# The second mixer's windowed attention: two heads at a time in the row and column halves of TensorE

## The chip, the cores and the metric

The kernel runs on one core of one Trainium2 chip. The metric is the time of one execution on the device, in microseconds (us). A core has TensorE (matrix products, PE in the profile), VectorE (DVE), ScalarE (ACT), GpSimd (POOL) and SyncE (SP, which here only issues the loads of weights). Each engine runs its instructions in its own order and waits on semaphores for the others. Operands lie in SBUF, matrix products are written to PSUM, which has 8 banks of 512 float32 columns on 128 partitions.

## What is computed

A two-layer hybrid backbone over 512 latent tokens and 256 context tokens, width 1024, in float32. Each layer is a gated feed-forward block, a mixer and a second feed-forward block, each modulated and residual. Layer 0's mixer is a Mamba-2 scan beside a dense multi-head attention. Layer 1's mixer, the one this case is about, is a windowed attention: 16 query heads and 4 key/value heads of width 64, a window of 128 tokens to either side, all 256 context keys, and one learned logit ("sink") per head in the softmax.

```python
def window_attend(q, k, v, kc, vc, sink, scale):
    # q (b,n,hk,r,d), k/v (b,n,hk,d), kc/vc (b,lc,hk,d), sink (hk,r); blocks of QBLK = 128 queries
    band = jnp.abs(qi[:, None] + WINDOW - kj[None, :]) <= WINDOW
    def block(i):
        ...
        s_loc = jnp.einsum("bqhrd,bkhd->bhrqk", qb, kb).astype(F32) * scale
        s_loc = jnp.where(valid, s_loc, -jnp.inf)
        s_ctx = jnp.einsum("bqhrd,bkhd->bhrqk", qb, kc).astype(F32) * scale
        prob = jax.nn.softmax(jnp.concatenate([s_loc, s_ctx, sink_l], axis=-1), axis=-1)
        return (jnp.einsum("bhrqk,bkhd->bqhrd", prob[..., :span], vb)
                + jnp.einsum("bhrqk,bkhd->bqhrd", prob[..., span:span + lc], vc))
```

## The kernel before

The program is written out engine by engine, in one fixed order of stages: feed-forward, first mixer (projection items, dense attention, scan), feed-forward twice, second mixer, feed-forward, output. The order in each engine's queue is the order in which the functions are called for that engine, and every dependence is a semaphore written by hand. Activations lie with their features on the partitions: a tile of 128 features x 768 tokens (512 latent, then 256 context).

The second mixer has four steps. `pe_items`, `act_items` and `dve_items` make keys (`gk`, 2 blocks of 128 features, so two heads to a block) and queries (`gq`, 8 blocks) with their norms and the rotary embedding; `pe_v_o` makes the values `gv` with tokens on the partitions; `pe_attend`, `act_attend` and `dve_attend` do the attention; `pe_out` is the output projection, which waits until all of the attention's outputs are written. GpSimd and SyncE have nothing to do in the attention.

The attention runs over 64 units: 16 heads x 4 blocks of 128 queries, `qt` = 0 to 3. A unit of `qt` 1 or 2 reads 640 keys (256 of the context and three blocks of 128), here called a middle unit; one of `qt` 0 or 3 reads 512, an edge unit. A query block of `gq` holds head i in partitions 0 to 63 and head i + 4 in 64 to 127, as their key heads lie in `gk`. The two halves are not used together: each unit takes one head.

For unit q the work goes round all three engines:

- TensorE, L1213: scores, 64 partitions contracted, into one of two pairs of PSUM banks. A float32 product stands in the profile as two records.
- VectorE, L1268: adds one or two masks of 128 columns to the scores; L1272: the row maximum; L1276 and L1278: scale, compare with the sink, negate.
- ScalarE, L1242: the exponential with its row sum, into `prob`; L1246: the exponential of the sink.
- VectorE, L1288, L1291, L1293: sum, reciprocal, scaling of `prob`.
- TensorE, L1222: four or five transposes of 128 x 128 into a pair of banks; ScalarE, L1259: one copy of them to `probT`.
- TensorE, L1231: the values, 64 columns out, into one half of the partitions of bank 6 or 7; ScalarE, L1252: rounded copy `go_hi`; VectorE, L1299: remainder `go_lo`.

The three engines hold four units at a time. In its turn q, TensorE issues the scores of q, the transposes of q-2 and the values of q-3. ScalarE issues the exponential of q, the sink of q, `go_hi` of q-3 and the copy of q-2. VectorE issues masks, maximum and the two small operations of q, then the sum, reciprocal and scaling of q-1, then `go_lo` of q-3.

## Time and profile before

| | |
|---|---|
| median of 3 runs | 3572.6 us (3569.13 to 3574.8) |
| the profiled execution's own time | 3573.73 us |
| its span, first to last instruction | 3571.9 us |
| mean granted TensorE clock | 0.971 |
| TensorE, VectorE, ScalarE, GpSimd busy | 94%, 47%, 28%, 8% of the span |

The span is the profiled execution; 1.8 us of its time lie around it. The page lists busy time by engine, the span in 40 slices, the DMA queues, the chain of work that ended last, and the costliest groups of instructions. "L1213" is line 1213 of the kernel before. In a timeline a row is one instruction, or several alike in a row (x5), with its start and its duration from first start to last end.

### The profile page before, as it was taken

What the parts mean: (1) busy time and instruction counts of PE and PEld (TensorE: products, weight loads), DVE (VectorE), ACT (ScalarE), POOL (GpSimd) and SP (SyncE); (2) the same over time, 40 slices, a digit from 0 to 9 for tenths busy, and PEclk for the clock granted to TensorE, in tenths of its full rate; (3) what the DMA queues carried; (4) which work ended last, traced back from release to release, by engine and by line L of the source; (5) the groups of instructions that cost most, each with busy time, mean ns of one, the idle gap of its engine ahead of it and who ended that gap; (6) DMA issues with size and microseconds to landing.
All of it is one profiled execution on the core that took longest, in us unless ns stands there. A gap on an engine that the chain in (4) does not pass through costs nothing.

```text
span 3571.9 us, 44734 instructions
## 1 busy us (share of the span) xinstructions
PE 3366.4 (94%) x18291; PEld 3039.5 (85%) x18291; DVE 1663.5 (47%) x2539; ACT 988.7 (28%) x1477; POOL 272.9 (8%) x310
## 2 busy tenths in 40 slices
PE   4999999989999989989999999999999988889999
PEld 3999999976779875578999999999999866668887
DVE  5643526435443626646623255432235457743333
ACT  2211212355431311133112113211212435532222
POOL 0100000200000015621000001000000000000000
PEclk9999999999999999999999999999999989999999
DMA  4533424401013210013523242322233210023332
GB/s 168 153 112 95 124 65 130 124 26 49 1 49 88 61 46 1 1 30 115 156 59 99 67 134 61 100 80 62 61 93 108 62 37 1 1 60 100 89 94 94
DMA packets 390047, 272.92 MB, mean 76 GB/s; under 512 B 33922, under 2 KB 365945, under 8 KB 389753
## 3 DMA queue, kind: packets, MB, share of 16 engines
q1 hardware_dynamic: 364537, 182.50, 17.7%
q0 software_dynamic: 25344, 88.09, 8.0%
q8 instruction: 119, 1.95, 0.2%
q14 instruction: 47, 0.39, 0.0%
HBM read 262.16 MB, written 8.39 MB: 76 GB/s over the span
## 4 chain that ended last, share of the span: by engine, by line
PE 52%; DVE 3%; ACT 2%; issue 1%; POOL 0%; ACTq 0%; DVEq 0%
PE ps L448 46%; PE ps L656 1%; PE ps L1213 1%; DVE stat L1272 1%; PE ps L1231 1%; PE ps L1585 1%; PE ps L1222 1%; PE ps L1100 1%; ACT prob L1242 0%; DVE ps L1268 0%; POOL xs L1628 0%; DVE w_lo L438 0%; ACT probT L1259 0%; PE ps L1559 0%; DVE h_sb L896 0%
## 5 line engine op out<-in xcount | busy, mean ns | idle before, releaser
L448 PE MATMUL ps<-u_hi,w_hi 128*128 128x384 f32 (+2 forms) x2992 | 833.0, 348 | 43.9 <-DVE w_lo L438 24.6
L438 DVE TENSOR_TENSOR w_lo<-ring,w_hi 128x1024 fp32r<-128x1024 f32 (+3 forms) x357 | 414.9, 1165 | 900.4 <-ACT w_hi L423 707.6
L448 PE MATMUL ps<-u_lo,w_hi 128*128 128x384 f32 (+2 forms) x2992 | 824.8, 345 | 0.0
L448 PE MATMUL ps<-u_hi,w_lo 128*128 128x384 f32 (+2 forms) x2992 | 824.0, 345 | 0.0
L448 PEld LDWEIGHTS ps<-u_hi,w_hi 128*128 128x128 f32 x2992 | 544.3, 191 | 74.7 <-issue 47.0
L448 PEld LDWEIGHTS ps<-u_lo,w_hi 128*128 128x128 f32 x2992 | 544.9, 190 | 22.6 <-issue 1.7
L448 PEld LDWEIGHTS ps<-u_hi,w_lo 128*128 128x128 f32 x2992 | 544.2, 190 | 21.5
L423 ACT CAST w_hi<-ring 128x1024 fp32r<-128x1024 f32 (+3 forms) x229 | 221.5, 968 | 1052.5 <-PE ps L448 1004.1
L448 PE MATMUL ps<-hid_hi,w_hi 128*128 128x384 f32 (+1 forms) x1232 | 343.6, 349 | 0.0
L448 PE MATMUL ps<-hid_lo,w_hi 128*128 128x384 f32 (+1 forms) x1232 | 342.9, 348 | 0.0
L448 PE MATMUL ps<-hid_hi,w_lo 128*128 128x384 f32 (+1 forms) x1232 | 342.0, 347 | 0.0
L626 DVE SCALAR_TENSOR_TENSOR m_sum<-m_in,sc,m_sum 128x1024 f32<-128x1024 f32 x224 | 277.1, 1279 | 6.0 <-DMA m_in<-in_w_mod 5.9
L430 ACT CAST w_hi<-ring 128x1024 fp32r<-128x1024 f32 x128 | 134.2, 1049 | 375.8 <-PE ps L448 375.8
L448 PEld LDWEIGHTS ps<-hid_lo,w_hi 128*128 128x128 f32 x1232 | 229.4, 192 | 6.8
L448 PEld LDWEIGHTS ps<-hid_hi,w_lo 128*128 128x128 f32 x1232 | 229.1, 192 | 6.8
L448 PEld LDWEIGHTS ps<-hid_hi,w_hi 128*128 128x128 f32 x1232 | 228.3, 192 | 6.9
L777 DVE TENSOR_TENSOR hid_f<-hid_f,ps 128x768 f32<-128x768 f32 x66 | 63.0, 955 | 313.0 <-PE ps L448 310.1
L896 DVE SCALAR_TENSOR_TENSOR h_sb<-ps,mod,h_sb 128x384 f32<-128x384 f32 (+3 forms) x296 | 135.1, 506 | 130.3 <-PE ps L448 130.1
L620 POOL DMA_DIRECT2D m_in<-in_w_mod x128 | 67.9, 530 | 1563.3 <-DVE m_sum L626 749.8
L758 ACT ACTIVATE hid_f<-ps 128x768 f32<-128x768 f32 x66 | 53.8, 815 | 431.9 <-PE ps L448 431.9
L1242 ACT ACTIVATE prob<-ps,stat 128x768 f32<-128x768 f32 (+3 forms) x112 | 83.9, 749 | 186.4 <-DVE stat L1278 105.5
L1222 PE MATMUL ps<-cst,prob 128*128 128x128 f32 x512 | 78.1, 281 | 34.4 <-ACT probT L1259 33.5
(250 smaller groups left out, 3678.0 us busy)
## 6 DMA issues: line engine op xcount, KB each, us to landing
ring<-in_w_ff_in SPq DMA_DIRECT2D x176, 512.0 KB, 3.8
m_in<-in_w_mod POOLq DMA_DIRECT2D x128, 512.0 KB, 4.0
ring<-in_w_ff_out SPq DMA_DIRECT2D x64, 512.0 KB, 3.6
ring<-in_w_in_e SPq DMA_DIRECT2D x26, 512.0 KB, 3.8
ring<-in_w_ff_out SPq DMA_DIRECT2D x32, 384.0 KB, 3.1
m_first<-in_w_mod POOLq DMA_DIRECT2D x16, 512.0 KB, 12.0
ring<-in_w_out_e SPq DMA_DIRECT2D x16, 512.0 KB, 3.7
...
```

The costliest lines, as they stand in the source:

```text
L423: act.copy(w_hi[:, (n % 2) * SLOT:(n % 2) * SLOT + WIDE[n]], ring[:, (n % RING) * SLOT:(n % RING) * SLOT + WIDE[n]]).then_inc(w_split_hi, 1)
L430: act.copy(w_hi[:, (n % 2) * SLOT:(n % 2) * SLOT + SLOT], ring[:, (n % RING) * SLOT:(n % RING) * SLOT + SLOT]).then_inc(w_split_hi, 1)
L438: dve.tensor_tensor(w_lo[:, b:b + WIDE[n]], ring[:, s:s + WIDE[n]], w_hi[:, b:b + WIDE[n]], ALU.subtract).then_inc(w_split_lo, 1)
L448: mm = pe.matmul(ps_at(p, c0, c1) if halved else pair(p)[:, c0:c1], w, x[:, c0:c1], start=start and i == 0, stop=stop and i == 2)
L620: pool.dma_start(m_in[:, D * (n % 2):D * (n % 2) + D], mod_src(x, k)).then_inc(m_full[n % 2], 16)
L626: x = dve.scalar_tensor_tensor(out=at_, in0=w, scalar=by, in1=at_, op0=ALU.mult, op1=ALU.add)
L656: mm = pe.matmul(bank(first + slot_, c0, c0 + 1), m_sum[:, D * (2 * slot_ + s) + P * d:D * (2 * slot_ + s) + P * d + P], ones[:, 0:1], sta ...
L758: act.activation(two(hid_f[:, jj, :]), halves(jj), ACT.Silu).then_inc(f_silu, 1)
L777: return dve.tensor_tensor(two(hid_f[:, q, :]), two(hid_f[:, q, :]), halves(2 + q), ALU.mult)
L896: x = dve.scalar_tensor_tensor(out=h[:, d, t0:t1], in0=pair(d % 2)[:, t0:t1] if whole else ps_at(d % 2, t0, t1), scalar=mod_group(g)[:, 2, ...
L1222: mm = pe.transpose(pair(2)[:, P * k:P * k + P], prob[:, i % 3, P * k:P * k + P], ident)
L1242: act.activation(prob[:, q % 3, :x["n"]], pair(q % 2, 1024)[:, :x["n"]], ACT.Exp, bias=stat[:, 4 + q % 4:5 + q % 4], scale=x["scale"], acc ...
```

## The change

The attention of the second mixer gets functions of its own. It takes two heads at a time, x = 0 to 7 being heads 2x and 2x + 1, which share a key head (x // 2), so there are 32 units `WU` instead of 64, each with 640 or 512 keys for each of its two heads:

- `gq` is loaded with its blocks in plain order, so one transfer for a block instead of two; head 2x lies in partitions 0 to 63, head 2x + 1 in 64 to 127.
- `gk` has four blocks: each holds one key head twice, in both halves of the partitions. GpSimd makes the copies (`pool_keys`), six of 64 x 768.
- `pe_window`: score products alternate between the halves, head 0 from rows 0 to 63, head 1 from rows 64 to 127. A unit's scores take three banks (two sets of three for two units). The tables `tiles`, `order` and `first` lay the columns so that products of both halves that follow each other write different banks; where both write the middle bank, one waits for the other (`wn_tail`).
- The transposes of both heads (8 or 10) go in rounds of four through one bank, bank 6, which ScalarE empties after each round. Between the rounds TensorE issues products with the values, alternating between the column halves 0 to 63 and 64 to 127, into one bank, bank 7.
- `act_window`: a unit's copies to `gpt` (2 or 3), then an exponential for each head, one for both sinks, then one `go_hi` of 128 x 128.
- `dve_window`: one addition of the masks for both heads (2 x 128 or 2 x 256 columns), one maximum over both heads' scores, the small operations on two columns, the scaling of the first head's probabilities alone, and one `go_lo` of 128 x 128.
- `pool_window`: GpSimd scales the second head's probabilities.

TensorE in the steady state, two turns before (`at_ex` is signalled by the exponential, `at_pn` by the scaling, `at_pt` by the copy `probT`, `at_o` by `go_lo`):

```order
L1213 MATMUL ps<-gk,gq 128x256 [waits at_ex]
L1213 MATMUL ps<-gk,gq 128x256
L1213 MATMUL ps<-gk,gq 128x128
L1222 MATMUL ps<-cst,prob 128x128 [waits at_pt,at_pn]
L1222 MATMUL ps<-cst,prob 128x128 x3
L1231 MATMUL ps<-probT,gv 64x128 [waits at_o,at_pt]
L1231 MATMUL ps<-probT,gv 64x128 x4
L1213 MATMUL ps<-gk,gq 128x256 [waits at_ex]
```

The transposes of a unit stand in one block, with one wait for a copy. One turn of the change (`wn_pt` by a copy to `gpt`, `wn_lo` by `go_lo`, `wn_n0` and `wn_n1` by the scalings of VectorE and GpSimd):

```order
L1321 MATMUL ps<-gk,gq 128x256 [waits wn_ex]
L1321 MATMUL ps<-gk,gq 128x256 x3
L1344 MATMUL ps<-cst,gp 128x128 [waits wn_n0,wn_pt,wn_lo]
L1344 MATMUL ps<-cst,gp 128x128 x3
L1357 MATMUL ps<-gpt,gv 64x128 x4
L1344 MATMUL ps<-cst,gp 128x128 [waits wn_pt,wn_n1]
L1344 MATMUL ps<-cst,gp 128x128 x3
L1357 MATMUL ps<-gpt,gv 64x128 x4
L1344 MATMUL ps<-cst,gp 128x128 [waits wn_pt]
L1344 MATMUL ps<-cst,gp 128x128
L1321 MATMUL ps<-gk,gq 128x256 [waits wn_ex]
```

The transposes of a unit, one block before, now stand in two or three blocks with values between them, and each block waits for a copy of ScalarE. The first of them also waits for the `go_lo` of the turn before.

ScalarE in the steady state, one turn before (middle unit; the first row is the exponential):

```order
L1242 ACTIVATE prob,stat<-ps,stat 128x640 [waits at_tr,at_nm]
L1246 ACTIVATE stat<-sink,stat 128x1
L1252 CAST go_hi<-ps 64x128 [waits at_pv]
L1259 COPY probT<-ps 128x512 [waits at_pv,at_tr]
L1242 ACTIVATE prob,stat<-ps,stat 128x640 [waits at_tr,at_nm]
```

One copy stands behind `go_hi`. The same in the change (the copies come before the exponentials of the turn):

```order
L1372 COPY gpt<-ps 128x512 [waits wn_pv,wn_tr]
L1372 COPY gpt<-ps 128x512 [waits wn_tr]
L1372 COPY gpt<-ps 128x256 [waits wn_tr]
L1381 ACTIVATE gp,gst<-ps,gst 128x512 [waits wn_tr,wn_nm]
L1381 ACTIVATE gp,gst<-ps,gst 128x512
L1385 ACTIVATE gst<-gst 128x2 [waits wn_sk]
L1389 CAST go_hi<-ps 128x128 [waits wn_pv]
```

The single copy behind `go_hi` has become two or three copies ahead of two exponentials, each of which waits for a round of transposes.

The diff's core. In the tables of loads and keys:

```diff
-        gq, gk, gv = at("gq", 16 * T, 8 * T), at("gk", 24 * T, 2 * T), at("gv", 26 * T, NT * 256)
+        gq, gk, gv = at("gq", 16 * T, 8 * T), at("gk", 24 * T, 4 * T), at("gv", 28 * T, NT * 256)
...
-            c0 = HD * (8 * (i // 4) + i % 4)
-            return lambda s: [(slot(s, 8)[:, :, 64 * e:64 * e + 64],
-                               w_ino[:, :, c0 + 4 * HD * e:c0 + 4 * HD * e + 64]) for e in range(2)]
+            return block(w_ino, 0, 8, P * i)
...
-            pe_attend(pe, n_mla, len(units))
-            pe.wait_ge(at_o, len(units))
+            pe.wait_ge(kk_two, 6)
+            pe_window(pe)
+            pe.wait_ge(wn_lo, NWU)
...
             pool_squares(pool, 4)
+            pool_keys(pool)
+            pool_window(pool)
             pool_squares(pool, 5)
```

The new functions:

```diff
+        for x in range(8):
+            for qt in range(SEQ // P):
+                lo, hi = max(0, qt - 1), min(3, qt + 1)
+                if hi - lo == 2:
+                    tiles = ([4, 5, qt - 1, qt + 1, qt], [qt, 4, 5, qt - 1, qt + 1])
+                    order = [(0, 4, 1), (1, 1, 2), (0, 0, 2), (1, 3, 1), (0, 2, 1), (1, 4, 1), (0, 3, 1), (1, 0, 1)]
+                    first, mask = (0, 896), (256, C_MP, 256)
+                else:
+                    tiles = ([4, 5, lo, hi], [4, 5, lo, hi])
+                    order = [(0, 0, 2), (1, 0, 2), (0, 2, 2), (1, 2, 2)]
...
+        def pool_keys(pool):
+
+            for b in range(2):
+                pool.wait_ge(hn_fin, items[n_even + b]["nrope"] + 1)
+                pool.wait_ge(hn_n, items[n_even + b]["norm"] + 1)
+                for e in range(2):
+                    pool.tensor_copy(gk[64 * e:64 * e + 64, 2 * b + 1, :], gk[64:128, 2 * b, :]).then_inc(kk_two, 1)
+                pool.wait_ge(kk_two, 3 * b + 2)
+                pool.tensor_copy(gk[64:128, 2 * b, :], gk[0:64, 2 * b, :]).then_inc(kk_two, 1)
+
+        def pool_window(pool):
+            for u in range(NWU):
+                n = WU[u]["n"]
+                pool.wait_ge(wn_ri, u + 1)
+                pool.tensor_scalar(gp[:, u % 3, n:2 * n], gp[:, u % 3, n:2 * n], gst[:, u % 4, 6, 1:2], None,
+                                   ALU.mult).then_inc(wn_n1, 1)
...
+        def pe_window(pe):
+            for u in range(NWU + 3):
+                if u < NWU:
+                    x = WU[u]
+                    g, q0 = x["g"], x["q0"]
+                    if u >= 2:
+                        pe.wait_ge(wn_ex, 2 * u - 2)
+                    for e, j, m in x["order"]:
+                        c = x["first"][e] + P * j
+                        k0 = P * x["tiles"][e][j]
+                        r = slice(64 * e, 64 * e + 64)
+                        if x["tail"] and (e, j) == (1, 0):
+                            pe.wait_ge(wn_tail, x["tail"])
+                        mm = pe.matmul(win(u, c, c + P * m), gq[r, x["x"], q0:q0 + P], gk[r, g, k0:k0 + P * m],
+                                       start=True, stop=True)
+                        if x["tail"] and (e, j) == (0, 4):
+                            mm.then_inc(wn_tail, 1)
+                    mm.then_inc(wn_sc, 1)
+                todo = list(range(WU[u - 3]["n"] // P)) if u >= 3 else []
+                if todo:
+                    y = WU[u - 3]
+                    pe.wait_ge(wn_pt, y["r0"] + y["nr"])
+                    if u >= 4:
+                        pe.wait_ge(wn_lo, u - 3)
+                i = u - 2
+                if 0 <= i < NWU:
+                    x = WU[i]
+                    nt = 2 * x["n"] // P
+                    for r in range(x["nr"]):
+                        if r == 0:
+                            pe.wait_ge(wn_n0, i + 1)
+                        if 4 * r + 4 > nt // 2 and (r == 0 or 4 * r <= nt // 2):
+                            pe.wait_ge(wn_n1, i + 1)
+                        if x["r0"] + r:
+                            pe.wait_ge(wn_pt, x["r0"] + r)
+                        for k in range(4 * r, min(nt, 4 * r + 4)):
+                            mm = pe.transpose(bank(6)[:, P * (k % 4):P * (k % 4) + P], gp[:, i % 3, P * k:P * k + P], ident)
+                        mm.then_inc(wn_tr, 1)
+                        if r < x["nr"] - 1:
+                            pe_window_values(pe, u - 3, todo[:2])
+                            todo = todo[2:]
...
+        def pe_window_values(pe, u, js):
+            for j in js:
+                y = WU[u]
+                nk = y["n"] // P
+                for e in range(2):
+                    k, c = y["tiles"][e][j], y["n"] * e + P * j
+                    mm = pe.matmul(bank(7)[64 * e:64 * e + 64, 0:P], gv[:, k, HD * y["g"]:HD * y["g"] + HD],
+                                   gpt[:, u % 2, c:c + P], start=j == 0, stop=j == nk - 1)
+                if j == nk - 1:
+                    mm.then_inc(wn_pv, 1)
+
+        def act_window(act):
+            for u in range(NWU + 3):
+                i = u - 2
+                if 0 <= i < NWU:
+                    x = WU[i]
+                    for r in range(x["nr"]):
+                        act.wait_ge(wn_tr, x["r0"] + r + 1)
+                        if r == 0 and i >= 2:
+                            act.wait_ge(wn_pv, i - 1)
+                        c0, c1 = 512 * r, min(2 * x["n"], 512 * r + 512)
+                        act.copy(gpt[:, i % 2, c0:c1], bank(6)[:, 0:c1 - c0]).then_inc(wn_pt, 1)
+                if u < NWU:
+                    x = WU[u]
+                    n = x["n"]
+                    act.wait_ge(wn_nm, u + 1)
+                    if u >= 3:
+                        act.wait_ge(wn_tr, WU[u - 3]["r0"] + WU[u - 3]["nr"])
+                    for e in range(2):
+                        c = x["first"][e]
+                        act.activation(gp[:, u % 3, n * e:n * e + n], win(u, c, c + n), ACT.Exp,
+                                       bias=gst[:, u % 4, 2, e:e + 1], scale=HD ** -0.5,
+                                       accum_out=gst[:, u % 4, 4, e:e + 1]).then_inc(wn_ex, 1)
+                    act.wait_ge(wn_sk, u + 1)
+                    act.activation(gst[:, u % 4, 5, :], gst[:, u % 4, 3, :], ACT.Exp).then_inc(wn_es, 1)
+                if u >= 3:
+                    y = WU[u - 3]
...
+        def dve_window(dve):
+            for u in range(NWU + 3):
+                if u < NWU:
+                    x = WU[u]
+                    f = gst[:, u % 4]
+                    dve.wait_ge(wn_sc, u + 1)
+                    c0, mk, w = x["mask"]
+                    s = win(u, 0, 1536).rearrange("p (b n) -> p b n", n=512)[:, 0:3:2, c0:c0 + w]
+                    dve.tensor_tensor(s, c_(mk, w).rearrange("p (o n) -> p o n", o=1).broadcast_to([P, 2, w]), s,
+                                      ALU.add).then_inc(wn_mk, 1)
+                    dve.wait_ge(wn_mk, u + 1)
+                    c = x["first"][1]
+                    s = win(u, 0, 2 * c).rearrange("p (b n) -> p b n", n=c)[:, :, 0:x["n"]]
+                    dve.tensor_reduce(f[:, 0, :], s, AX, ALU.max).then_inc(wn_mx, 1)
+                    sk = sink[:, 2 * x["x"]:2 * x["x"] + 2]
+                    dve.wait_ge(wn_mx, u + 1)
+                    dve.scalar_tensor_tensor(out=f[:, 1, :], in0=f[:, 0, :], scalar=HD ** -0.5, in1=sk,
+                                             op0=ALU.mult, op1=ALU.max).then_inc(wn_m, 1)
+                    dve.wait_ge(wn_m, u + 1)
+                    dve.tensor_scalar(f[:, 2, :], f[:, 1, :], -1.0, None, ALU.mult).then_inc(wn_nm, 1)
+                    dve.tensor_tensor(f[:, 3, :], sk, f[:, 1, :], ALU.subtract).then_inc(wn_sk, 1)
+                i = u - 1
+                if 0 <= i < NWU:
+                    f, n = gst[:, i % 4], WU[i]["n"]
+                    dve.wait_ge(wn_ex, 2 * i + 2)
+                    dve.wait_ge(wn_es, i + 1)
+                    dve.tensor_tensor(f[:, 4, :], f[:, 4, :], f[:, 5, :], ALU.add).then_inc(wn_l, 1)
+                    dve.wait_ge(wn_l, i + 1)
+                    dve.reciprocal(f[:, 6, :], f[:, 4, :]).then_inc(wn_ri, 1)
+                    dve.wait_ge(wn_ri, i + 1)
+                    dve.tensor_scalar(gp[:, i % 3, 0:n], gp[:, i % 3, 0:n], f[:, 6, 0:1], None, ALU.mult).then_inc(wn_n0, 1)
+                if u >= 3:
+                    y = WU[u - 3]
+                    o = slice(y["q0"], y["q0"] + P)
+                    dve.wait_ge(wn_hi, u - 2)
+                    dve.tensor_tensor(go_lo[:, y["x"], o], bank(7, 0, P), go_hi[:, y["x"], o], ALU.subtract).then_inc(wn_lo, 1)
```

## Rows read from the trace of the kernel before

**Rows 1.** The page: busy time and share of the span, chain by line

```profile
PE 3366.4 (94%) x18291; PEld 3039.5 (85%) x18291; DVE 1663.5 (47%) x2539; ACT 988.7 (28%) x1477; POOL 272.9 (8%) x310
...
PE ps L448 46%; PE ps L656 1%; PE ps L1213 1%; DVE stat L1272 1%; PE ps L1231 1%; PE ps L1585 1%; PE ps L1222 1%; PE ps L1100 1%; ACT prob L1242 0%; DVE ps L1268 0%; POOL xs L1628 0%; DVE w_lo L438 0%; ACT probT L1259 0%; PE ps L1559 0%; DVE h_sb L896 0%
```

**Rows 2.** The tiles gq and go_lo: first and last score product, first and last output

```profile
L1213 PE MATMUL ps<-gk,gq x320: 269/376/793, 2916.4 to 3131.7; 64*128 64x256 f32 x128, 64*128 64x128 f32 x32
...
L1299 DVE TENSOR_TENSOR go_lo<-ps,go_hi x64: 282/288/295, 2929.7 to 3143.2; 64x128 fp32r<-64x128 f32 x64
```

**Rows 3.** Chain of waits, 2890 to 3160 us: start us, us, what

```profile
by line: PE ps L1213 12.1%; DVE stat L1272 11.9%; PE ps L1231 11.8%; issue 10.8%; PE ps L1222 7.2%; PE ps L1100 7.0%; ACT prob L1242 6.4%; DVE ps L1268 6.3%; PE ps L448 6.2%; ACT probT L1259 4.3%; DVE stat L1276 3.3%; ACT go_hi L1252 3.2%; 
...
3001.05 1.24 PE ps L1231 x10
...
3055.26 1.24 PE ps L1231 x10
```

**Rows 4.** Timeline, one middle unit: start us, us, engine, line, op, operands

```profile
3005.43 0.80 ACT L1242 ACTIVATE prob<-ps,stat 128x640 f32<-128x640 f32 x1 [2.00 <-DVE stat L1278]
...
3006.22 0.28 ACT L1246 ACTIVATE stat<-sink,stat 128x1 f32<-128x1 f32 x1
3006.52 0.26 ACT L1252 CAST go_hi<-ps 64x128 fp32r<-64x128 f32 x1
3006.81 0.59 ACT L1259 COPY probT<-ps 128x512 f32<-128x512 f32 x1
3006.82 0.29 DVE L1299 TENSOR_TENSOR go_lo<-ps,go_hi 64x128 fp32r<-64x128 f32 x1 [0.62 <-ACT go_hi L1252]
3007.14 0.49 DVE L1268 TENSOR_TENSOR ps<-cst,ps 128x128 f32<-128x128 f32 x2
...
3007.54 0.63 PE L1222 MATMUL ps<-cst,prob 128*128 128x128 f32 x4 [0.82 <-ACT probT L1259]
3007.67 0.82 DVE L1272 TENSOR_REDUCE stat<-ps 128x1 f32<-128x640 f32 x1
...
3008.10 1.09 PE L1231 MATMUL ps<-probT,gv 128*64 128x128 f32 x8
3008.53 0.21 DVE L1276 TENSOR_SCALAR stat<-stat,sink 128x1 f32<-128x1 f32 x1
...
3008.96 0.80 ACT L1242 ACTIVATE prob<-ps,stat 128x640 f32<-128x640 f32 x1 [1.57 <-DVE stat L1278]
```

**Rows 5.** Groups by line and form, 2950 to 3100 us: busy us, mean ns

```profile
L1272 DVE TENSOR_REDUCE stat<-ps 128x1 f32<-128x640 f32 x23 | 19.0, 824 | 0.8
...
L1272 DVE TENSOR_REDUCE stat<-ps 128x1 f32<-128x512 f32 x22 | 15.2, 691 | 0.8
...
L1242 ACT ACTIVATE prob<-ps,stat 128x512 f32<-128x512 f32 x22 | 15.1, 688 | 29.4 <-DVE stat L1278 29.4
```

**Rows 6.** Timeline of TensorE in the SSD stage, heads in both column halves

```profile
1361.88 0.42 PE L1585 MATMUL ps<-ee,st 128*64 128x128 f32 x1
1361.94 0.42 PE L1585 MATMUL ps<-mf,xdt 128*64 128x128 f32 x1
1362.10 0.42 PE L1585 MATMUL ps<-ee,st 128*64 128x128 f32 x1
1362.16 0.42 PE L1585 MATMUL ps<-ee,xdt 128*64 128x128 f32 x1
```

**Rows 7.** Stretches: from:to, us, busy us (count) of each engine, PEclk, DMA

```profile
1360.70:1364.10 3.40, 3.40 (x29) 3.40 (x28) 2.73 (x4) 0.00 (x0) 0.37 (x1) 0.50 0.00 0
...
1537.00:1558.00 21.00, 12.74 (x43) 7.01 (x42) 9.80 (x11) 12.36 (x15) 6.92 (x4) 1.00 0.00 0
2915.00:2934.00 19.00, 16.89 (x53) 12.37 (x54) 12.16 (x40) 6.34 (x18) 0.00 (x0) 0.56 0.01 3
2934.00:3140.00 206.00, 179.21 (x1120) 137.72 (x1119) 152.17 (x507) 108.23 (x299) 0.00 (x0) 1.00 0.00 1
```

**Rows 8.** Groups by line and form, GpSimd, whole span

```profile
L499 POOL TENSOR_TENSOR acc<-acc,sqn 128x512 f32<-128x512 f32 x5 | 6.4, 1288 | 18.7 <-ACT sqn L490 18.7
```

84 lines of the change are left out of this document (33 added, 51 removed).

## The prediction

> **What bounds the kernel now.** The page comes first [rows 1]. TensorE is busy for 94% of the span, and the chain that ended last is made of its dense products (L448, 46%); VectorE is at 47%. That is an average over stages, and says nothing of the stage that changes. Its ends are in [rows 2]: the first score product starts at 2916.4 us, the last `go_lo` at 3143.2, and 0.3 later it ends, so the attention takes 227.1 us, 6% of the span. The output projection waits for it, so each microsecond gained there is one of the end.
>
> In that stage the chain goes from engine to engine [rows 3]: scores 12.1%, maximum 11.9%, values 11.8%, transposes 7.2%, exponential 6.4%, with the masks, copies and small operations between them. From 3001.05 to 3055.26 the pattern repeats after 16 units: 54.21 us, 3.39 us a unit. 64 units make 216.8 us, and filling, emptying and the first products at a low clock make the other 10.3.
>
> One middle unit shows what the 3.39 consist of [rows 4]. From exponential to exponential: the exponential starts at 3005.43, the sink 0.79 later, `go_hi` 0.30 later, `go_lo` 0.30, the masks 0.32, the maximum 0.53, L1276 0.86, and the next exponential 0.43 later, at 3008.96. That is 3.53 us without a gap: ScalarE waits for VectorE's maximum, VectorE for ScalarE's `go_hi`. The same sum for an edge unit is 3.09, and the mean of both 3.31 against 3.39 measured, so this way of adding is some 2% short. TensorE is close behind the loop: busy for 179.21 of 206 us [rows 7].
>
> **What the change removes and adds, per pair of heads.** Two old units cost 6.78 us. The work that is now done once for two heads, from the nearest rows:
>
> - Masks, one operation of 512 columns (middle) or 256 (edge). A subtraction from PSUM takes 0.29 us for 128 columns (`go_lo` [rows 4]), and the maximum 0.133 more for each further 128 [rows 5]: 0.69 for 512 and 0.42 for 256. Before, two pairs of 0.49 (middle).
> - Maximum over 1280 or 1024 columns. 0.691 for 512 and 0.824 for 640 [rows 5] give 1.04 ns a column: 1.49 and 1.22 us. Only the fixed part of one is saved.
> - Two small operations, the sink's exponential, `go_hi` and `go_lo`, each once instead of twice, at 0.15 to 0.30 each [rows 4]. I take the same price for the wider forms: two masks on 128 partitions take 0.49 together, no more than two `go_lo` on 64 would [rows 4]. The other bound is twice these, some +1 us a pair; no row speaks for it.
> - The exponentials stay two: 2 x 0.79 (middle) or 2 x 0.68 (edge, from 0.688 [rows 5]).
>
> This gives a first leg, from the start of `go_hi` to the next exponential over VectorE: middle 0.30 + 0.32 + 0.73 + 1.53 + 0.43 = 3.31 us, edge 0.30 + 0.32 + 0.46 + 1.26 + 0.43 = 2.77 (0.04 is the gap behind each of masks and maximum).
>
> **The wait that takes its place.** Before, one copy of 0.59 us (edge) emptied the transposes, and it stood off the loop. Now all pass one bank in rounds of four, and ScalarE must do the two or three copies before it may do the turn's exponentials. The first round waits on TensorE for `go_lo` of the turn before. So there is a second leg from the same `go_hi`: `go_lo` starts 0.30 later and takes 0.29; a product of TensorE starts 0.14 behind the copy that it waits for (3006.81 + 0.59 to 3007.54 [rows 4]); four transposes take 0.63; 0.04 to the copy; the copy of 512 columns takes 0.59 [rows 4]. To here 1.99 us. A second round is 0.14 + 0.67 + 0.59 = 1.40, and a third of two transposes and 256 columns 0.14 + 0.45 + 0.37 = 0.96, where 0.37 is 0.59 less twice the 0.11 by which exponentials of 640 and 512 columns differ [rows 4, 5]. The leg takes 3.39 us where the copies are those of an edge pair and 4.35 for a middle pair. It is longer than the first leg each time, so ScalarE now waits for transposes and not for the maximum.
>
> A turn is this leg, two exponentials and 0.30 for the sink. The copies belong to the pair two before the one whose exponentials come next, so the four kinds of turn are: edge exponentials, edge copies 1.66 + 3.39 = 5.05; middle, edge 1.88 + 3.39 = 5.27; middle, middle 1.88 + 4.35 = 6.23; edge, middle 1.66 + 4.35 = 6.01. Together 22.56 us for four pairs, 5.64 a pair, and 180.5 for 32.
>
> Both ends: the pipeline is three turns deep as before, and 10.3 us stood there. The turns are longer and fewer, the low clock at the start stays; I take 7, between 4 (no low clock) and 10.3. **The stage takes 187 us instead of 227, 40 less.**
>
> **TensorE in a turn.** Column halves overlap in the scan's stage [rows 6]: L1585 makes heads in both halves, and products of two chains alternate there while each chain advances by 0.22 us, at the low clock (1360.70 to 1364.10, PEclk 0.50 [rows 7]). One chain alone, the values L1231, takes 1.09 us for eight records at the full clock [rows 4], 0.11 to 0.12 each once the last has started, and twice that at the low one. So the second chain is free. I take the same for the row halves, which no row shows: scores 1.1 us, values 10 records of two at 0.11, transposes 1.1, and six changes of shape of about 0.1: 3.9 us in a middle turn of 5.3 to 6.2. That is off the bound.
>
> The Trainium skill, "TensorE: Matmul & The Clock Gate", part 3, says that small products in different row groups start within 4 ns of each other and run together, as those in different column groups do; no row here has it for rows. By that rule the sum is the same.
>
> **GpSimd.** Its scaling of 640 columns has one input where GpSimd's addition has two, which takes 1.29 us for 512 columns [rows 8]: between half of that and 1.29 x 640 / 512 = 1.61 us. It is needed only by the second round of transposes a turn later, so it costs nothing. The six copies of keys, 768 columns, take at most 1.5 x 1.29 = 1.9 each and run under the projection of the queries, where GpSimd is idle; cost 0, at most some 2 us if VectorE is held up. The loads of `gq` become one transfer for two; SyncE's queue there waits for slots, not for data: 0. Outside the attention nothing else moves.
>
> **The sum.** 3573.7 - 40 = 3533.7 for the profiled execution. The median shown is 1.1 lower, which gives **3533 us**.
>
> **Rivals.**
>
> 1. *The row halves, or both kinds, run one after another.* TensorE then needs 2.2 for scores, 1.1 for transposes, 2.2 for values and 0.6 for changes of shape, 6.1 us in a middle pair and 5.0 in an edge pair, about what the turns have. Each block of values between rounds takes 0.87 + 0.2 instead of 0.43 + 0.2, 0.1 us beyond the copy it lies under, and the scores come later for the masks. Some 9 us: 3542. Against it stand [rows 6], for columns only.
> 2. *VectorE and GpSimd hold each other up.* Both scalings start at the same reciprocal. No row shows VectorE slowed by GpSimd. If it waits out a whole scaling of up to 1.61 us, the slack between the small operations and `go_lo` (1.88 + 0.30 + 0.18, less 1.1 of its own work, so 1.2) leaves up to 0.4 us a turn, 12 us: 3545. The Trainium skill, "SBUF — State Buffer", section "Summary: rules for kernel authors", speaks for this: of a VectorE instruction in a two-port mode and GpSimd, the second to issue is blocked until the first ends. By it VectorE, which waits for its own signal, would mostly go first.
> 3. *The clock stays low through the stage.* The row of 2915 to 2934 has PEclk 0.56, one of 1.2 GHz for most of it, at the same thin start of the pipeline. TensorE would need 2.1 for scores, 2.1 for transposes, 2.1 for values and 0.6 for changes of shape, 6.9 us in a middle pair and 5.7 in an edge pair, and part of each wait for a round's copy comes on top: about 6.8 a pair, 218 and the ends 7, 225 us: 3571, no difference. Against it: from 1537 to 1558 TensorE is busy for 12.74 of 21 us and keeps the full clock [rows 7]; the turns above give 3.9 of 5.6, more than that.
> 4. *The other side: each change of half costs what a change of shape costs.* The values start 0.56 after four transposes of 0.11 [rows 4], so a change of shape costs 0.12. A middle pair has 7 changes of half in its scores and 9 in its values, an edge pair 3 and 7. With nothing overlapped TensorE needs 6.1 + 1.9 = 8.0 and 5.0 + 1.2 = 6.2 us, 7.1 a pair, 227 us, and with ends 234: 3580, slower. It decides from 0.10 us a change on, where TensorE's 5.55 + 13 x 0.10 passes the old time of a pair. Against it: in [rows 6] an alternation costs nothing.
>
> **How the numbers follow.** Forecast 0.73; rival 1 0.09; rival 2 0.07; rival 3 0.05; rival 4 0.03; 0.03 for a stage shorter than 178 us, if rounds hand over faster than 0.14 + 0.04. 0.2% of this kernel, 7 us, is about what a measurement can tell from no change. Faster takes all but rivals 3 and 4 and a bit more: 0.91; within 0.2% 0.06; slower 0.03. The forecast's own range is the 2% of the sum in either direction, 3 to 6 us at the ends and 2 for the keys: 3526 to 3541. Reaching to rivals 1 and 2: 3524 to 3547.
>
> **What the profile afterwards would show.** The attention from its first score to its last `go_lo` takes 183 to 191 us. Four pairs (two heads, all queries) repeat every 22.6 us. ScalarE's copies to `gpt` wait for TensorE's transposes, about 0.8 us before each second copy, and the exponentials wait little for `gst`. Maximum 1.22 and 1.49 us, masks 0.42 and 0.69. Score products of one half start while the other's run. GpSimd's scaling is under 1.6 us. Wrong would be: exponentials that wait for the maximum (then the first leg binds, and the price of the rounds is smaller than I say), scores of a middle pair taking 2.2 us (rival 1), VectorE's scaling much over half a microsecond (rival 2), PEclk at 0.5 past the first 20 us (rival 3).

## The result, and the profile after

The changed kernel takes **3520.24 us** (median of 4 runs, 3519.51 to 3522.98) beside 3570.86 (4 runs, 3567.36 to 3574.8) for the kernel before. The ratio is 0.9859, with a 95% interval of 0.9842 to 0.9876. That is 51 us less where 40 were forecast, and below the low end of the range, 3524. The profiled execution took 3522.98, its span 3520.8.

The page of the kernel after, the rows that answer to [rows 1]: busy time by engine, and the chain that ended last, by line.

```profile
PE 3303.5 (94%) x18355; PEld 2983.3 (85%) x18355; DVE 1604.3 (46%) x2283; ACT 971.2 (28%) x1429; POOL 344.9 (10%) x348
...
PE ps L457 72%; PE ps L1193 2%; PE ps L665 2%; PE ps L1711 1%; PE ps L1344 1%; PE ps L1211 1%; PE ps L1109 1%; PE ps L1321 1%; ACT gpt L1372 1%; DVE w_lo L447 1%; PE ps L1685 1%; PE ps L1202 1%; DMA u_sb<-in_ctx 1%; PE ps L1004 1%; PE ps L1686 1%
```

In the chain the new stage's transposes L1344, scores L1321 and copies L1372 have 1% each; the page says no more of one stage. The tiles `gq` and `go_lo` give its ends, as in [rows 2] (engine, operation, count: shortest, median and longest ns, first and last start).

```profile
L1321 PE MATMUL ps<-gk,gq x384: 269/376/792, 2916.6 to 3074.4; 64*128 64x128 f32 x98, 64*128 64x256 f32 x94
```

```profile
L1426 DVE TENSOR_TENSOR go_lo<-ps,go_hi x32: 290/292/293, 2934.9 to 3092.0; 128x128 fp32r<-128x128 f32 x32
```

From 2916.6 to 3092.3 the attention takes **175.7 us**, where it took 227.1 and I had forecast 187. The spans differ by 51.1 and the stage by 51.4: everything happened inside the stage, and it also began at the same time (2916.4 and 2916.6), so the keys' copies and the new loads cost nothing that shows.

The chain of waits, 2890 to 3110 us, by line, answers to [rows 3]:

```profile
by line: PE ps L1344 22.8%; issue 16.4%; PE ps L1321 14.3%; ACT gpt L1372 12.7%; PE ps L1109 8.5%; PE ps L457 8.1%; PE ps L1357 5.6%; ACT gp L1381 4.9%; DVE go_lo L1426 1.5%; ACT go_hi L1389 1.0%; DVE gv L1161 0.9%; DVE gst L1404 0.6%; DVE 
```

Before, the maximum stood at the head with the scores and values (11.9%). Now it has 0.6%, and the transposes with their copies have 35.5%. The list of waits for 2940 to 3080 us (engine, line and what it waited for: us in total, times, longest) says the same from the other side:

```profile
ACT gpt L1372 <- PE ps L1344: 58.2, 67, 1.1
```

ScalarE stands 58.2 of 140 us before its copies. No wait of the exponential L1381 for the maximum is in the list. One turn, from exponential to exponential, answers to [rows 4]; both its exponentials and its copies are those of edge pairs:

```profile
3001.38 0.69 ACT L1381 ACTIVATE gp<-ps,gst 128x512 f32<-128x512 f32 x1
...
3002.05 0.69 ACT L1381 ACTIVATE gp<-ps,gst 128x512 f32<-128x512 f32 x1
...
3002.72 0.21 ACT L1385 ACTIVATE gst<-gst 128x2 f32<-128x2 f32 x1
3002.81 0.27 ACT L1389 CAST go_hi<-ps 128x128 fp32r<-128x128 f32 x1
3003.11 0.29 DVE L1426 TENSOR_TENSOR go_lo<-ps,go_hi 128x128 fp32r<-128x128 f32 x1 [2.43 <-ACT go_hi L1389]
...
3003.50 0.63 PE L1344 MATMUL ps<-cst,gp 128*128 128x128 f32 x4 [0.76 <-issue]
3004.04 1.49 DVE L1404 TENSOR_REDUCE gst<-ps 128x2 f32<-128x1280 f32 x1
...
3004.17 0.58 ACT L1372 COPY gpt<-ps 128x512 f32<-128x512 f32 x1 [1.09 <-PE ps L1344]
...
3004.90 0.63 PE L1344 MATMUL ps<-cst,gp 128*128 128x128 f32 x4 [0.18 <-ACT gpt L1372]
...
3005.56 0.59 ACT L1372 COPY gpt<-ps 128x512 f32<-128x512 f32 x1 [0.81 <-PE ps L1344]
3005.76 0.17 DVE L1410 TENSOR_SCALAR gst<-gst 128x2 f32<-128x2 f32 x1
...
3006.05 0.80 ACT L1381 ACTIVATE gp<-ps,gst 128x640 f32<-128x640 f32 x1
```

Against the forecast's turn of 5.05 us:

| step, from start to start | forecast | measured |
|---|---|---|
| two exponentials, to the sink | 1.36 | 1.34 |
| sink to `go_hi` | 0.30 | 0.09 |
| `go_hi` to the first transposes | 0.73 | 0.69 |
| transposes to copy | 0.67 | 0.67 |
| copy to the second round's transposes | 0.73 | 0.73 |
| transposes to copy | 0.67 | 0.66 |
| last copy to the next exponential | 0.59 | 0.49 |
| sum | 5.05 | 4.67 |

The other three kinds of turn, read in the same way, take 4.88 (forecast 5.27), 5.78 (6.23) and 5.57 (6.01). Four pairs take 20.89 us instead of 22.56; over 32 pairs that is 13.4 us. The ends took 8.6 us instead of 7. The difference, 11.8, is what the stage was shorter than the forecast's 187.5.

The wide operations, by line and form from 2950 to 3080 us (busy us, mean ns | idle before), answer to [rows 5] and [rows 8]; the last fence is GpSimd:

```profile
L1404 DVE TENSOR_REDUCE gst<-ps 128x2 f32<-128x1280 f32 x12 | 17.9, 1490 | 0.4
L1404 DVE TENSOR_REDUCE gst<-ps 128x2 f32<-128x1024 f32 x13 | 15.9, 1224 | 0.4
L1399 DVE TENSOR_TENSOR ps<-cst,ps 128x512 f32<-128x512 f32 x12 | 8.2, 685 | 0.0
...
L1399 DVE TENSOR_TENSOR ps<-cst,ps 128x256 f32<-128x256 f32 x13 | 5.5, 419 | 0.0
```

```profile
L1305 POOL TENSOR_SCALAR gp<-gp,gst 128x640 f32<-128x640 f32 x14 | 31.4, 2242 | 35.9 <-DVE gst L1419 35.9
L1305 POOL TENSOR_SCALAR gp<-gp,gst 128x512 f32<-128x512 f32 x12 | 22.3, 1856 | 45.4 <-DVE gst L1419 45.4
```

Maximum 1490 and 1224 ns, masks 685 and 419: the forecast had 1.49, 1.22, 0.69 and 0.42. GpSimd needs 2.24 us for 640 columns, outside the bound of 1.61. The stretches (from:to, us, busy us of PE, PEld, DVE, ACT, POOL, then PEclk) answer to [rows 7]:

```profile
2930.00:2940.00 10.00, 8.28 (x77) 5.67 (x76) 4.90 (x16) 5.88 (x16) 4.10 (x2) 0.94 0.01 2
2940.00:3080.00 140.00, 105.91 (x1040) 74.36 (x1038) 88.53 (x243) 81.81 (x229) 55.00 (x27) 1.00 0.00 1
```

The granted clock stays at 2.4 GHz from 2940 on. TensorE is busy for 105.91 of 140 us, so it has room; that the stage is a chain of handovers is what e3 and b1 put to the test.

### The profile page after: what moved, and what is told of

The parts are those of the page before. It is cut to its first block, busy times and chain, and to the rows that moved or that the text cites. A ratio compares the mean times of both kernels' runs of the same rounds, so it can differ in the third digit from the quotient of the medians.

```text
span 3520.8 us, 44458 instructions
## 1 busy us (share of the span) xinstructions
PE 3303.5 (94%) x18355; PEld 2983.3 (85%) x18355; DVE 1604.3 (46%) x2283; ACT 971.2 (28%) x1429; POOL 344.9 (10%) x348
## 4 chain that ended last, share of the span: by engine, by line
PE 88%; ACT 4%; DVE 4%; issue 2%; POOL 1%; DMA 1%; SPq 1%; ACTq 0%; DVEq 0%
PE ps L457 72%; PE ps L1193 2%; PE ps L665 2%; PE ps L1711 1%; PE ps L1344 1%; PE ps L1211 1%; PE ps L1109 1%; PE ps L1321 1%; ACT gpt L1372 1%; DVE w_lo L447 1%; PE ps L1685 1%; PE ps L1202 1%; DMA u_sb<-in_ctx 1%; PE ps L1004 1%; PE ps L1686 1%
## 5 line engine op out<-in xcount | busy, mean ns | idle before, releaser
L1344 PE MATMUL ps<-cst,gp 128*128 128x128 f32 x288 | 49.7, 293 | 39.1 <-issue 20.1
L1305 POOL TENSOR_SCALAR gp<-gp,gst 128x512 f32<-128x512 f32 (+1 forms) x32 | 65.5, 2048 | 167.8 <-DVE gst L1419 167.8
```

Source lines behind the costliest of these rows:

```text
L1305: pool.tensor_scalar(gp[:, u % 3, n:2 * n], gp[:, u % 3, n:2 * n], gst[:, u % 4, 6, 1:2], None, ALU.mult).then_inc(wn_n1, 1)
L1344: mm = pe.transpose(bank(6)[:, P * (k % 4):P * (k % 4) + P], gp[:, i % 3, P * k:P * k + P], ident)
```

## The experiments

Two questions were open. Is the gain what I said it is, the round of waits ScalarE, TensorE, ScalarE in place of two units' loops, with TensorE's halves overlapping? And why was each turn 0.4 us shorter than its sum? Turn lengths below are for the four kinds in the order edge exponentials with edge copies, middle with edge, middle with middle, edge with middle: after has 4.67, 4.88, 5.78, 5.57 = 20.89. e1 to e4 ran beside one set of runs of the kernel before (median 3572.03), e5 to e7 and b1 beside another (3573.06).

### e1: the scores of both heads in one row half

```diff
-                        r = slice(64 * e, 64 * e + 64)
+                        r = slice(0, 64)
```

The second head's scores are made from the first head's queries; the amount of work is the same.

> Of the kernel after, both heads' score products contract partitions 0 to 63 (the second head's scores are then those of the first; the same instructions, shapes and waits). Theory (the two row halves run together, and TensorE is off the bound): the 16 score records of a middle pair grow from 1.37 us to about 2.2, the stage of 175.5 us grows by 0 to 10 us, since TensorE has slack in a turn. Rival (row halves never overlapped, the shorter stage has another cause): scores stay at 1.37 us and the time stays within 2 us of 3520.

Measured: 3534.81 us, ratio 0.9897 (0.9881 to 0.9914), 14.6 more than the change. Turns 5.15, 5.18, 5.77, 5.57 = 21.67. TensorE's timeline of e1 and, under it, the same row of the kernel after:

```profile
3008.71 2.47 PE L1321 MATMUL ps<-gk,gq 64*128 64x128 f32 x16
```

```profile
3006.26 1.37 PE L1321 MATMUL ps<-gk,gq 64*128 64x128 f32 x16
```

A middle pair's 16 records take 2.47 us in one row half and 1.37 in two. So the row halves do overlap, which no row of before could show. In one half the next record starts 0.11 us after one of 128 columns and 0.22 after one of 256, so the time goes with the columns and not with the number of weight loads; it is the products that overlap. The Trainium skill ("TensorE: Matmul & The Clock Gate", part 3) says so, with about 4 ns between starts, and the single records of the change agree with it: from 3007.02 us on those of the two halves start in pairs, 4 to 7 ns apart, and the pairs 0.11 us apart. From the first start to the last it is 1.10 us in the change and 2.19 in e1, which are the 1.1 and 2.2 that I had; the rows add the last record's own 0.27. The stage grew by more than the 10 us that were expected at most.

Of the stage's 12.7 us (188.4 instead of 175.7), 6.2 are the turns' 0.78 x 8 and 6.2 the filling: the first `go_lo` starts 24.5 us after the first score in e1, and 18.3 in the change. At the start TensorE is at 1.2 GHz for a while. The stretches of e1, and under them those of the change and of e5 (further down), where TensorE does the same as in the change:

```profile
2917.00:2930.00 13.00, 12.23 (x45) 10.23 (x44) 8.18 (x21) 3.98 (x12) 1.85 (x1) 0.50 0.00 0
2930.00:2940.00 10.00, 9.66 (x42) 6.48 (x42) 3.51 (x10) 5.27 (x15) 4.49 (x2) 0.67 0.00 0
```

```profile
2917.00:2930.00 13.00, 10.71 (x61) 8.04 (x58) 9.60 (x23) 6.11 (x17) 4.09 (x2) 0.52 0.00 0
```

```profile
2917.00:2930.00 13.00, 8.30 (x68) 6.49 (x68) 11.05 (x27) 6.27 (x18) 3.52 (x2) 0.87 0.01 3
```

In e1 TensorE is busy there almost without a gap (12.23 of 13 us), so the longer scores lengthen the filling. But the clock has a part in it too: it is back at 2.4 GHz later in e1 than in the change (0.67 against 0.94 for 2930 to 2940), and in e5 it was back early, with 16.2 us of filling. So some 2 us of a filling can differ without any change in TensorE's work, and how the 6.2 divide between scores and clock is not shown.

### e2: the values in one column half as well

```diff
-                    mm = pe.matmul(bank(7)[64 * e:64 * e + 64, 0:P], gv[:, k, HD * y["g"]:HD * y["g"] + HD],
-                                   gpt[:, u % 2, c:c + P], start=j == 0, stop=j == nk - 1)
+                    mm = pe.matmul(bank(7)[0:64, 0:P], gv[:, k, HD * y["g"]:HD * y["g"] + HD],
+                                   gpt[:, u % 2, c:c + P], start=True, stop=True)
```

On top of e1. The values of both heads are written over each other and not summed.

> As e1_rows, and both heads' products with the values go to the column half 0 as well, each product for itself (the sum over the key blocks is left out, and half of the outputs are stale). Theory: values between two rounds of transposes (8 records) grow from 0.66 to about 1.1 us, longer than the copy of 0.59 that they lie under, so each second round comes up to 0.3 us later: with the scores some 5 to 20 us over the kernel after, 3525 to 3540. If the whole gain of the change came from the overlap in the halves (rival), this kernel is back at 3560 to 3571.

Measured: 3552.28 us, ratio 0.9947 (0.993 to 0.9964), 32.0 more than the change. Turns 5.38, 6.04, 6.30, 6.05 = 23.77.

```profile
3002.71 1.99 PE L1321 MATMUL ps<-gk,gq 64*128 64x256 f32 x8
3004.63 0.65 PE L1344 MATMUL ps<-cst,gp 128*128 128x128 f32 x4
3005.21 1.09 PE L1357 MATMUL ps<-gpt,gv 128*64 128x128 f32 x8
3006.23 0.66 PE L1344 MATMUL ps<-cst,gp 128*128 128x128 f32 x4
```

```profile
ACT gpt L1372 <- PE ps L1344: 69.2, 60, 2.0
...
DVE ps L1399 <- PE ps L1321: 12.2, 18, 1.1
```

Eight records of values take 1.09 us instead of 0.66, and each stands between two rounds of transposes: the round's period goes from 1.40 (3003.50 to 3004.90 in the change) to 1.60 (3004.63 to 3006.23). The masks now wait for scores, 12.2 us in all. TensorE, busy for 105.91 us between 2940 and 3080 in the change, is now busy for 137.46 of these 140: it has become the bound of the stage, which the expected 3525 to 3540 did not foresee. In this order of the work the overlap in both halves is worth 32 of the 51 us; without it the change would have gained about 20.

### e3: the wait for `go_lo` behind the first round of transposes

The values of a unit must wait until `go_lo` of the one before has read bank 7. The change has that wait ahead of the transposes, which don't use that bank.

```diff
-                    if u >= 4:
-                        pe.wait_ge(wn_lo, u - 3)
...
+                if j == 0 and u >= 1:
+                    pe.wait_ge(wn_lo, u)
```

> Of the kernel after, TensorE waits for the last go_lo in front of the first product with the values instead of in front of the first round of transposes. Theory (the leg through the rounds sets the turn): the first round runs while go_hi and go_lo are made; the legs go_hi to exponential of now 3.24 us (edge copies) and 4.15 (middle copies) fall to about 3.1 (VectorE's leg) and 3.5, some 1.5 us in four pairs, 12 us in all, up to 16: 3505 to 3509. Rival (VectorE's leg sets the turn, as before the change): no difference, 3520.

Measured: 3506.08 us, ratio 0.9818 (0.9802 to 0.9835), 14.2 less than the change. Turns 4.59, 4.79, 4.95, 4.75 = 19.08; 8 x 1.81 = 14.5. The timeline of e3, one turn:

```profile
3000.36 0.78 ACT L1381 ACTIVATE gp<-ps,gst 128x640 f32<-128x640 f32 x1
...
3000.56 0.63 PE L1342 MATMUL ps<-cst,gp 128*128 128x128 f32 x4 [0.60 <-issue]
...
3001.23 0.26 ACT L1389 CAST go_hi<-ps 128x128 fp32r<-128x128 f32 x1
3001.37 0.60 ACT L1372 COPY gpt<-ps 128x512 f32<-128x512 f32 x1
...
3001.86 0.66 PE L1357 MATMUL ps<-gpt,gv 128*64 128x128 f32 x8 [0.67 <-DVE go_lo L1426]
...
3003.15 0.59 ACT L1372 COPY gpt<-ps 128x512 f32<-128x512 f32 x1 [1.18 <-PE ps L1342]
```

```profile
ACT gpt L1372 <- PE ps L1342: 35.2, 43, 1.2
...
PE ps L1357 <- DVE go_lo L1426: 14.0, 20, 0.7
...
ACT gp L1381 <- DVE gst L1410: 8.2, 13, 0.6
```

The first round's transposes now run during the exponentials, and the copy follows `go_hi` at once. So the leg by `go_lo` and the transposes was indeed what set the turn. Nearly all of the gain lies in the two turns with middle copies (0.83 and 0.82 us); those with edge copies lose only 0.08 and 0.09, because the leg over VectorE's maximum lies right below and takes over. The other leg doesn't vanish either: the second round now stands behind values that wait for `go_lo` (14.0 us), and exponentials that did not wait for the maximum in the change now do (8.2).

### e4: the kernel before, with `go_hi` and `go_lo` on all 128 partitions

In the unit of [rows 4] the output of an odd head is written, which starts at partition 64. Where it is an even head's, in the same trace, the gaps are shorter: sink to `go_hi` 0.18 instead of 0.30, `go_hi` to copy 0.15 instead of 0.29, `go_lo` to masks 0.21 instead of 0.32. The edit lets every output start at partition 0, at the same number of columns, and with it the part of bank 6 or 7 that is read for it:

```diff
-                                  out=tuple(x[64 * (hh % 2):64 * (hh % 2) + 64, hh // 2, q0:q0 + P]
+                                  out=tuple(x[:, hh // 2, q0:q0 + P]
...
-                    act.copy(x["out"][0], bank(6 + i % 2)[x["o"]:x["o"] + x["m"], 0:P]).then_inc(at_oh, 1)
+                    act.copy(x["out"][0], bank(6 + i % 2)[:, 0:P]).then_inc(at_oh, 1)
...
-                    dve.tensor_tensor(x["out"][1], bank(6 + i % 2)[x["o"]:x["o"] + x["m"], 0:P], x["out"][0],
+                    dve.tensor_tensor(x["out"][1], bank(6 + i % 2)[:, 0:P], x["out"][0],
```

Two heads' outputs are written over each other.

> Of the kernel before, go_hi and go_lo of every head are written as 128 partitions from partition 0 on, instead of 64 from partition 0 or 64 (half of the outputs are then overwritten with other values). Theory (an instruction whose output starts in another part of the partitions than the last one's waits until the last has ended, which lengthened the unit of an odd head that the sum was read from): in odd heads' units sink to go_hi falls from 0.31 to 0.19 us, go_lo to the masks from 0.33 to 0.21, even heads' units stay; the kernel is 3 to 8 us faster than before. Rival (the gaps belong to odd units for another reason, or the wider operations are simply dearer): no difference, or slower.

Measured: 3568.74 us, ratio 0.9989 (0.998 to 0.9999). The same unit as in [rows 4], on ScalarE and on VectorE:

```profile
3005.59 0.80 ACT L1242 ACTIVATE prob<-ps,stat 128x640 f32<-128x640 f32 x1 [2.01 <-DVE stat L1278]
...
3006.37 0.28 ACT L1246 ACTIVATE stat<-sink,stat 128x1 f32<-128x1 f32 x1
3006.55 0.25 ACT L1252 CAST go_hi<-ps 128x128 fp32r<-128x128 f32 x1
3006.70 0.59 ACT L1259 COPY probT<-ps 128x512 f32<-128x512 f32 x1
3008.86 0.80 ACT L1242 ACTIVATE prob<-ps,stat 128x640 f32<-128x640 f32 x1 [1.57 <-DVE stat L1278]
```

```profile
3006.84 0.29 DVE L1299 TENSOR_TENSOR go_lo<-ps,go_hi 128x128 fp32r<-128x128 f32 x1 [0.48 <-ACT go_hi L1252]
3007.05 0.48 DVE L1268 TENSOR_TENSOR ps<-cst,ps 128x128 f32<-128x128 f32 x2
```

The three gaps are now 0.18, 0.15 and 0.21, and the unit takes 3.27 us instead of 3.53. Units that write an even head's output stay as they were. Over all units the mean falls from 3.39 to 3.30, 5.8 us for 64, and the stage from 227.1 to 221.6; the medians show 3.3 of it, with an interval from 0.4 to 7. The operations themselves take as long as before, within 0.01 us.
### e5: the sink's exponential with a bias again

```diff
-                    act.activation(gst[:, u % 4, 5, :], gst[:, u % 4, 3, :], ACT.Exp).then_inc(wn_es, 1)
+                    act.activation(gst[:, u % 4, 5, :], gst[:, u % 4, 3, :], ACT.Exp,
+                                   bias=gst[:, u % 4, 2, 0:1]).then_inc(wn_es, 1)
```

The bias is the first head's negated maximum and changes the sinks' terms; it is there for its time alone.

> Of the kernel after, the sinks' exponential gets a bias from the statistics again, as the kernel before had it (the denominators are then wrong). Theory (the rest of the short gap sink to go_hi, 0.09 us after against 0.18 in even heads before, belongs to this operation's form): it takes 0.28 instead of 0.21 us, go_hi starts 0.18 instead of 0.09 behind it, each turn is 0.09 longer, the stage 3 us: 3523. Rival (the gap belongs to go_hi's own form): no difference, 3520.

Measured: 3528.17 us, ratio 0.9871 (0.9855 to 0.9888).

```profile
3003.46 0.30 ACT L1385 ACTIVATE gst<-gst 128x2 f32<-128x2 f32 x1
3003.65 0.27 ACT L1390 CAST go_hi<-ps 128x128 fp32r<-128x128 f32 x1
```

The exponential takes 0.30 instead of 0.21, and `go_hi` starts 0.19 behind it instead of 0.09. Each kind of turn is 0.09 longer (4.76, 4.97, 5.87, 5.66), 2.9 us in all; one single turn of the profiled execution took 6.53, for a reason that stays open. The medians differ by 7.9, where 3 were expected, but come from different sets of runs; the ratios, 0.9871 and 0.9859, have intervals that overlap, and the stage itself grew by 2.4 us. So 0.09 of the missing 0.21 at the sink are the bias of its exponential, and 0.12 the hold of e4.

### e6: VectorE scales both heads' probabilities

```diff
                     dve.tensor_scalar(gp[:, i % 3, 0:n], gp[:, i % 3, 0:n], f[:, 6, 0:1], None, ALU.mult).then_inc(wn_n0, 1)
+                    dve.tensor_scalar(gp[:, i % 3, n:2 * n], gp[:, i % 3, n:2 * n], f[:, 6, 1:2], None, ALU.mult).then_inc(wn_n1, 1)
...
-            pool_window(pool)
```

> Of the kernel after, VectorE scales the second head's probabilities too, and GpSimd has no part in the window. Theory (VectorE idles 1.1 to 2.4 us in front of go_lo, and GpSimd's scaling is needed only a turn later): no difference, within 2 us of 3520. Rival (the two scalings hold each other up): faster by 3 us or more. If VectorE had no slack: 0.5 us a turn, 16 us slower.

Measured: 3521.71 us, ratio 0.9857 (0.9841 to 0.9874): no difference. Turns 4.67, 4.88, 5.78, 5.57, as in the change. Groups of VectorE in e6, 2950 to 3080 us:

```profile
L1421 DVE TENSOR_SCALAR gp<-gp,gst 128x640 f32<-128x640 f32 x13 | 7.2, 554 | 0.5
L1422 DVE TENSOR_SCALAR gp<-gp,gst 128x640 f32<-128x640 f32 x13 | 7.1, 548 | 0.0
```

L1421 takes 554 ns with GpSimd's scaling beside it in the change, and 554 without it here. GpSimd does not slow VectorE here, and its 2.24 us gain nothing either: on VectorE the same work is also hidden.

### e7: masks and maximum per head

```diff
-                    dve.tensor_reduce(f[:, 0, :], s, AX, ALU.max).then_inc(wn_mx, 1)
+                    dve.tensor_reduce(f[:, 0, 0:1], s[:, 0, :], AX, ALU.max)
+                    dve.tensor_reduce(f[:, 0, 1:2], s[:, 1, :], AX, ALU.max).then_inc(wn_mx, 1)
```

The masks are split in the same way.

> Of the kernel after, masks and maxima are made for each head by itself, two operations of each instead of one. Theory: VectorE's leg (go_hi to exponential, some 3.12 us) grows by 0.2 to 0.3 us and passes the 3.24 us of the leg through the rounds in the two turns of four that begin middle exponentials, 0.1 to 0.2 each: 2 to 4 us slower, 3522 to 3524. Rival (one operation for two heads is what the change gains by): over 10 us slower.

Measured: 3524.21 us, ratio 0.9859 (0.9842 to 0.9875). Four turns take 20.98 us instead of 20.89, 0.7 us over the stage. The growth is in the two turns with edge copies, 0.05 and 0.04. From the masks to the small operation behind the maximum VectorE takes 2.37 us instead of 2.24, so the leg over the maximum had only 0.08 to spare there, the same 0.08 at which e3 stopped. That VectorE does the masks and the maximum of both heads in one operation is worth nothing measurable in this order of the work.

### b1: another order

The rest of the stage is handovers, so b1 keeps every operation and moves them. TensorE makes the scores one pair ahead, between the first and the second round of transposes; ScalarE puts its copies between the exponentials and does `go_hi` a turn later; VectorE does `go_lo` in the middle of its turn.

```diff
+            for u in range(-1, NWU + 3):
+                pe_round(pe, u - 2, 0)
+                pe_scores(pe, u + 1)
+                pe_round(pe, u - 2, 1)
...
+                pe_window_values(pe, u - 3, js[:2])
+                pe_round(pe, u - 2, 2)
+                pe_window_values(pe, u - 3, js[2:])
...
+                copy_round(u - 2, 0)
...
+                exponential(u, 0)
+                copy_round(u - 2, 1)
+                exponential(u, 1)
+                copy_round(u - 2, 2)
```

> The same operations as the kernel after in another order: TensorE issues the scores one pair ahead, between the first and second round of transposes; ScalarE puts the copies between the exponentials and makes go_hi at the start of the next turn, VectorE go_lo in the middle of its turn. Theory (what is left after the change is waiting for each other in turn, not work): no leg goes through all three engines any more, VectorE with about 4.1 us of work in a middle pair and 3.4 in an edge pair sets the turn; the stage falls from 175.5 us to 130 to 140, the time to 3475 to 3485. Rival (an engine's work is the bound): no faster than the variant with the moved wait, 3506.

Measured: **3476.68 us** (3473.41 to 3481.22), ratio 0.9734 (0.9718 to 0.975), 96 us less than the kernel before beside it. In the profiled execution (3473.41) the stage takes 133.2 us (2909.3 to 3042.5), 42.5 less than in the change, and a pair 3.84. The stages ahead of it ended 7 us earlier in that execution, which is no part of the edit; the medians differ by 43.6.

```profile
2940.00:3040.00 100.00, 96.27 (x995) 71.17 (x994) 78.92 (x220) 77.00 (x215) 52.09 (x26) 1.00 0.01 1
```

TensorE is now busy for 96.27 of 100 us and VectorE for 78.92. So the stage's 130 to 140 us were forecast rightly, but not what sets them: it was to be VectorE's work, and it is TensorE that is almost never free. How much each of the moves is worth was not taken apart. Of all kernels here this is the fastest; e3 beats the change too.

## Why the prediction was wrong, point by point

The direction and the mechanism held; the time did not, because terms of the turn were mis-sized. The sum gave 22.56 us for four pairs, and they took 20.89. The step that failed most is "and 0.30 for the sink".

- **What binds the stage: right.** A chain of handovers, not a busy engine. In the kernel before, two of the gaps that e4 shortens lie on the loop (0.12 and 0.11 us), and the unit became 0.26 shorter. But a loop of ScalarE and VectorE alone was not the whole of it: in half of its units the masks waited for TensorE's scores, as this line of its list of waits for 2950 to 3100 us shows.

```profile
DVE ps L1268 <- PE ps L1213: 8.5, 22, 0.6
```

- **The wait that takes its place: right, narrowly in half of the turns.** ScalarE waits for transposes (58.2 us) and not for the maximum. e3 takes the first round off the leg and gains 14.2 us. With edge copies the forecast had the two legs 0.08 us apart (3.39 and 3.31), and e3 and e7 find just this. e7 lengthens the first leg and loses 0.7 us of the stage.
- **The 0.30 for the sink: wrong, and the largest part of the error.** It was read from sink to `go_hi` in [rows 4], where an odd head's output is written, and carried to a change whose outputs all start at partition 0. It is 0.09: of the 0.21 between them, 0.12 are the hold (e4) and 0.09 the bias that the sink's exponential no longer has (e5). Times 32 pairs: 6.7 us.
- **The last copy's 0.59 before the exponential: wrong by 0.10.** I added whole durations where ScalarE's instructions start some 0.1 before the previous one ends. The kernel before has it too where nothing is held: in e4's rows `go_hi` starts at 3006.55 and the sink ends at 3006.65. Times 32: 3.2 us. This is read from the trace; no run took it apart.
- **Smaller ones, from the trace alone:** `go_hi` to the transposes 0.69 instead of 0.73, 1.3 us; the exponentials' spacing, about 1 us; a third round of two transposes, about 0.06 in every second turn, 1 us. Together with the two above this is 13.2 of the 13.4 us by which the turns were shorter.
- **The handovers between the rounds: right** (0.15 and 0.03 against 0.14 and 0.04). I gave 0.03 to a stage under 178 us, by faster handovers. The stage was under 178, but by other terms.
- **"This way of adding is some 2% short": the step that should have warned me.** That sum agreed with the mean period, and I took this as a test of its terms and gave the new turns the same 2%. The agreement was luck. From one exponential to the next, the trace of before has for `qt` 0 to 3 of a head 3.96, 3.53, 3.21 and 3.24 us where the first three write an odd head's output, and 3.71, 3.26, 2.93 and 3.26 where they write an even one's. The mean of these eight is 3.39. The sum had 3.53, which is one kind of eight, and 3.09 for an edge unit, which is none: those that begin with an edge exponential take 3.24 to 3.96. The holds that it put into every unit made up for the scores that come late, for which it had no term. The terms that I carried over were those of the slower kind, and the turns were off by 7.4%, to the other side.
- **The ends: 8.6 us, forecast 7.** Inside the stated 4 to 10.3, and they move with the clock at the start: the filling took 18.3 us in the change and 16.2 in e5.
- **Masks, maxima, wide copies: right** to 0.01 us. Small operations cost no more on two columns, as taken.
- **TensorE in a turn: right.** The scores of a middle pair take 1.10 us from first start to last, and 1.37 with the last record's end. The rows had shown only the overlap of column halves; that the row halves do the same was taken over, and e1 bears it out.
- **GpSimd: wrong price, right cost.** 2.24 us against a bound of 1.61 from an addition with two inputs: the multiplication with one wide input takes 1.86 us for 512 columns and that addition 1.29. Why is open; each of these multiplications also starts beside VectorE's scaling. It is hidden (e6).
- **Rival 1 (serial halves): did not happen, and was priced at 9 us.** e2, which makes it happen, costs 29.7 us of the stage. Its turns are nearly those of the rival, 5.94 us a pair against the forecast's 5.64 and 9 / 32 more, 5.92. What was wrong is what they were compared with: the change's own turns are 5.22 and not 5.64, so the loss against them is larger. The ends are wrong too, with 15.2 us in e2 against 7.
- **Rival 2 (VectorE and GpSimd): no.** 554 ns with and without GpSimd. The rule of the Trainium skill ("SBUF — State Buffer", section "Summary: rules for kernel authors") blocks the second to issue; VectorE's starts 0.06 us ahead (3000.19 and 3000.25 in the timeline of the change), and what GpSimd may lose by it is hidden, so no run here tells whether the rule acts. Each of GpSimd's scalings starts so, and none was measured alone.
- **Rival 3 (low clock): no**, 1.00 from 2940 on. **Rival 4 (a price for each change of half): no.** With 7 changes of half, a middle pair's scores take 1.37 us; without any, in e1, 2.47.
